# Two transformer blocks on one core: the first layer's modulation made per tile of x

## What is computed

```python
def _layer(x, c, positions, norm_g, w_ada, b_ada, w_in, ...):
    mod = jax.nn.silu(c) @ w_ada + b_ada
    shift, scale, gate = jnp.split(mod, 3, axis=-1)
    h = _rmsnorm(x, norm_g) * (1.0 + scale[:, None, :]) + shift[:, None, :]
    proj = h @ w_in
    (rq, rk, rv, rg, xbc, dt_raw, z, fq, fk, fv, fg, f_raw) = jnp.split(proj, IN_OFFSETS, axis=-1)
    ...
```

## Time and profile before

| | us |
|---|---|
| median of 3 runs | 3177.47 (3176.85 to 3179.08) |
| the profiled execution | 3176.42 |
| its span in the trace | 3174.6 |
| PE busy | 3070.6 |

### The profile page before, as it was taken

How to read it: one execution, slowest core, us unless ns; L and a number is a source line. 1 busy time by engine, 2 the same in 40 slices (tenths; PEclk the granted TensorE clock), 3 DMA queues, 4 the chain that set the end, 5 groups by cost and what they waited for, 6 DMA issues and landing times. The chain is left out here.

```text
span 3174.6 us, 39298 instructions
## 1 busy us (share of the span) xinstructions
PE 3070.6 (97%) x15352; PEld 2478.9 (78%) x15352; DVE 1241.9 (39%) x1997; ACT 928.7 (29%) x1623; POOL 1391.7 (44%) x1074
## 2 busy tenths in 40 slices
PE   8999999989999999999999999999999999999998
PEld 5887777778777788887767888878888776788886
DVE  8466244746433222222375322332222237532233
ACT  4356442435453211103463211021110346421101
POOL 2443445524343545445341544454444434154542
PEclk8999999999999999999999999999999999999999
DMA  6222315213231222232110222222222221022222
GB/s 262 100 82 105 101 57 210 103 67 113 87 110 40 73 101 92 85 97 95 67 41 28 93 97 93 91 90 101 98 85 92 86 80 41 28 92 93 88 91 72
DMA packets 45861, 287.78 MB, mean 91 GB/s; under 512 B 5496, under 2 KB 6008, under 8 KB 18680
## 3 DMA queue, kind: packets, MB, share of 16 engines
q1 hardware_dynamic: 42480, 270.32, 24.2%
q10 hardware_dynamic: 3240, 15.53, 1.5%
HBM read 283.67 MB, written 2.16 MB: 90 GB/s over the span
## 5 line engine op out<-in xcount | busy, mean ns | idle before, releaser
L1926 POOL TENSOR_TENSOR w_parts<-w_raw,w_parts 128x512 fp32r<-128x512 f32 (+1 forms) x544 | 703.2, 1321 | 752.9 <-DVE w_parts L2061 702.4
L1986 PE MATMUL PS<-x_parts,w_parts 128*128 128x512 f32 x4224 | 961.1, 390 | 4.5 <-ACT x_parts L799 4.5
L1986 PEld LDWEIGHTS PS<-x_parts,w_parts 128*128 128x128 f32 x4224 | 793.4, 188 | 173.7 <-issue 5.3
L139 POOL TENSOR_TENSOR w_parts<-w_raw,w_parts 128x512 fp32r<-128x512 f32 x380 | 532.6, 1432 | 820.4 <-ACT w_parts L128 790.6
L369 PE MATMUL PS<-x_parts,w_parts 128*128 128x512 f32 x2784 | 698.6, 397 | 14.8 <-POOL w_parts L139 13.7
L369 PEld LDWEIGHTS PS<-x_parts,w_parts 128*128 128x128 f32 x2784 | 521.2, 189 | 135.5 <-POOL w_parts L139 17.8
L2027 PE MATMUL PS<-hidden_parts,w_parts 128*128 128x512 f32 x2112 | 482.9, 390 | 0.0
L2027 PEld LDWEIGHTS PS<-hidden_parts,w_parts 128*128 128x128 f32 x2112 | 396.2, 188 | 83.8 <-issue 1.9
L2068 DVE TENSOR_TENSOR ffn_buffers<-PS,ffn_buffers 128x512 f32<-128x512 f32 x88 | 60.9, 692 | 732.1 <-PE PS L1986 708.9
L128 ACT CAST w_parts<-w_raw 128x2048 fp32r<-128x2048 f32 (+1 forms) x92 | 172.1, 1870 | 140.6 <-PE PS L369 52.3
L2061 DVE CAST w_parts<-w_raw 128x2048 fp32r<-128x2048 f32 (+1 forms) x144 | 156.9, 1089 | 113.4 <-PE PS L2027 113.4
(11 more groups left out here) (396 smaller groups left out, 3116.2 us busy)
## 6 DMA issues: line engine op xcount, KB each, us to landing
w_raw<-in_w_gu SPq DMA_DIRECT2D x88, 1024.0 KB, 4.7
w_raw<-in_w_in SPq DMA_DIRECT2D x70, 1024.0 KB, 4.8
w_raw<-in_w_d SPq DMA_DIRECT2D x64, 704.0 KB, 4.0
w_raw<-in_w_out SPq DMA_DIRECT2D x24, 1024.0 KB, 4.8
m_all<-in_w_next SPq DMA_DIRECT2D x14, 1024.0 KB, 8.2
m_all<-in_w_gate SPq DMA_DIRECT2D x8, 1024.0 KB, 4.8
ssd_buffers<-decay_rows ACTq DMA_DIRECT2D x16, 512.0 KB, 3.9
m_all<-in_w_next ACTq DMA_DIRECT2D x2, 1024.0 KB, 14.1
```

The source lines that it names most:

```text
L139: last = pool.tensor_tensor(parts[:, self.slot(u), 1, at:to], raw[:, self.slot(u), at:to], parts[:, self.slot(u), 0, at:to].bitcast(F32), ...
L1926: last = pool.tensor_tensor(WP[:, b, 1, at:to], RAW[:, b, at:to], WP[:, b, 0, at:to].bitcast(F32), ALU.subtract)
L1986: return pe.matmul(PS[:, 2 * b + g, :], WP[:, slot(b), w, c:c + P], XS[:, x, k, :], start=start, stop=stop)
```

## The change

Only the start of layer 0 changes; layer 1 goes on using `Modulated` and `begin`.

- The host lays the first-half weights of `w_ada` in layer 0 out anew: unit k now holds the shift and the scale of tile k of x. Units 0 to 2 (`TURNED` = 3) are stored the other way round for PE.
- Units 0 to 2 become products on PE (`product`): 16 matmuls of one column each per unit, with `c` as a column. Product 0 stands between the sums and `spread_inverse`, product 1 ahead of the first matmuls of jobs 0 and 1, product 2 ahead of those of the second tile.
- Units 3 to 7 stay dot products on DVE, now each ahead of its own tile, inside the loop over tiles.
- `begin_apart` begins four jobs on the arriving tiles: jobs 0 and 1 on tile n, jobs 2 and 3 on tile n - 3.
- The loads are ordered anew: x in two halves on both queues, c as a column and as a row, units 0 and 1 of `w_in` at once. The second `keep_busy` group and the two matmuls of `spread_inverse` go. The sines are made after the last tile.

```diff
-                self.spread_inverse(pe, 2)
-                keep_busy(pe, 2, 4)
+
+            def spread_inverse(self, pe):
+                pe.wait_ge(self.moved, 1)
+                for c in range(NT):
+                    last = pe.matmul(PS[:, RSTD, c * P:(c + 1) * P], stats[:, 8 + c:9 + c].broadcast_to([P, P]),
+                                     ident, start=True, stop=True)
+                last.then_inc(self.spread, 1)
...
+            def product(self, n):
+                def run(pe):
+                    pe.wait_ge(self.loaded[n], 16)
+                    if n == 0:
+                        pe.wait_ge(self.column_ready, 1)
+                    if n >= 2:
+                        pe.wait_ge(self.columns, 2 * (n - 1))
+                    for h in range(2):
+                        for k in range(KD):
+                            at = k * 2 * P + h * P
+                            last = pe.matmul(PS[:, self.bank(n), h:h + 1], self.ring[:, n, at:at + P],
+                                             self.c_column[:, k:k + 1], start=(k == 0), stop=(k == KD - 1))
+                    last.then_inc(self.products, 1)
+                return run
+
+            def vector(self, dve):
+                n = self.norm
+                dve.wait_ge(n.spread, 2)
+                for k in range(KD + 1):
+                    if k < KD:
+                        if k < TURNED:
+                            dve.wait_ge(self.products, k + 1)
+                            shift, scale = (PS[:, self.bank(k), h:h + 1] for h in range(2))
+                        else:
...
+                            dot_rows(dve, self.ring[:, k % 4, :], self.B.scratch, self.B.c_row,
+                                     raw_mod[:, 2 * k:2 * k + 2], self.used, 2 * m)
+                            dve.wait_ge(self.used, 2 * m + 2)
...
+                        dve.tensor_tensor(msb[:, k:k + 1], shift, p1("b_ada")[:, k:k + 1],
+                                          ALU.add).then_inc(self.columns, 1)
+                        dve.scalar_tensor_tensor(amul[:, k:k + 1], scale, msb[:, 8 + k:9 + k],
+                                                 p1("norm_g")[:, k:k + 1], ALU.add, ALU.mult).then_inc(self.columns, 1)
...
+                        dve.scalar_tensor_tensor(self.tile(k), X[:, k, :], amul[:, k:k + 1], PS[:, RSTD, :],
+                                                 ALU.mult, ALU.mult).then_inc(n.scaled, 1)
...
-                proj.begin(pe, (0, 1), before)
-                for j in range(2, nj):
+                if l:
+                    proj.begin(pe, (0, 1), before)
+                else:
+                    proj.begin_apart(pe, (((0, 1), 0), ((2, 3), 3)), before,
+                                     {n: before.product(n + 1) for n in range(TURNED - 1)})
+                for j in range(2 if l else 4, nj):
...
             def _(pe):
                 pe.wait_ge(s_in, 32)
                 norm.sums(pe, B.squares)
+                first.product(0)(pe)
+                norm.spread_inverse(pe)
...
+                act.dma_start(first.c_column, dr["c_column"]).then_inc(s_cc, 16)
                 act.dma_start(posi, dr["pos"]).then_inc(s_in, 16)
...
+                act.dma_start(x_all[:, half:2 * half], dr["x"][:, half:2 * half]).then_inc(s_x, 16)
+                act.dma_start(par[:, 0:P1N], of_layer("par1", 0)).then_inc(first.parameters, 16)
+                for u in range(2):
+                    act.dma_start(first.ring[:, u, :], ada_rows(0, u)).then_inc(first.loaded[u], 16)
+                act.dma_start(B.c_row, dr["c_row"]).then_inc(first.row_loaded, 16)
+                act.dma_start(first.ring[:, 2, :], ada_rows(0, 2)).then_inc(first.loaded[2], 16)
```

More of the change, by code:

```diff
@@ L316, in run_half, with begin_apart @@
                 last.then_inc(self.projected, 1)
+            def begin_apart(self, pe, groups, x, between):
+                for n in range(KD + 1 + max(lag for _, lag in groups)):
+                    if n in between:
+                        between[n](pe)
+                    for jobs, lag in groups:
+                        i = n - lag
+                        if 0 <= i < KD:
+                            pe.wait_ge(x.high, i + 1)
+                            for j in jobs:
+                                u, kind, c, m, ncols, kt = self.jobs[j]
+                                if i == 0:
+                                    pe.wait_ge(self.stream.low, u + 1)
+                                for a in range(2):
+                                    w = WP[:, self.stream.slot(u), a, 0:kt * ncols].rearrange("p (k n) -> p k n", k=kt)
+                                    pe.matmul(PS[0:m, self.bank(j), :], w[:, i, c:c + m], XS[:, 0, i, :],
+                                              start=(i == 0 and a == 0), stop=False)
+                        if 1 <= i <= KD:
+                            pe.wait_ge(x.low, i)
+                            for j in jobs:
+                                u, kind, c, m, ncols, kt = self.jobs[j]
+                                w = WP[:, self.stream.slot(u), 0, 0:kt * ncols].rearrange("p (k n) -> p k n", k=kt)
+                                last = pe.matmul(PS[0:m, self.bank(j), :], w[:, i - 1, c:c + m], XS[:, 1, i - 1, :],
+                                                 start=False, stop=(i == KD))
+                                if i == KD:
+                                    last.then_inc(self.projected, 1)
             def begin(self, pe, jobs, x, order=range(KD)):
@@ L2780, in mix_tokens, with setup @@
             return output
[L2783 to L2789, removed]
+        def setup(block, norm, B, first):
+            stream = first.stream
+            s_in, s_x = (sem(x) for x in ("constants_loaded", "x_loaded"))
+            s_cc = sem("c_column_loaded")
+            s_vc = sem("setup_vector_step")
@@ L2807, in _ @@
-                stream.send(sp, RAW, SLOTS)
-                sp.wait_ge(s_c1, 16)
+                    if u - 4 < TURNED:
+                        sp.wait_ge(first.products, u - 3)
+                    else:
+                        sp.wait_ge(first.used, 2 * (u - 3 - TURNED))
+                    sp.dma_start(first.ring[:, u % 4, :], ada_rows(0, u)).then_inc(first.loaded[u % 4], 16)
+                sp.dma_start(spec[:, 0:C1N], dr["c1"]).then_inc(first.constants, 16)
+                sp.wait_ge(first.constants, 16)
```

108 lines of the change are left out of this document (66 added, 42 removed).

## The result

| | before | changed |
|---|---|---|
| median of the runs, us | 3178.22 (3176.85 to 3179.08) | 3201.28 (3199.67 to 3204.27) |
| the profiled execution | 3176.42 | 3199.67 |
| its span | 3174.6 | 3197.9 |

The changed kernel is slower: the ratio is 1.0074, with a 95% interval of 1.0062 to 1.0087. The forecast was 3204, its range 3193 to 3212.

A forecast was written before the change was run, and what follows sets the result against it. PE, busy 97% of the span, was taken as the bound, so only the start mattered. Job 4 25.0 us later plus 2.0 of lost clock made 27.0; on 3176.4 plus 1.05 to the median, 3204 us, range 3193 to 3212.

The forecast's parts named there:

- The sum: Total predicted delay: job 4 starting 25.0 us later plus 2.0 us of lost clock, 27.0 us.
- Sums, products, spread at half clock: PE before tile 2: sums 11.57 us, each product 6.9 at 1.2 GHz, spread 2.08; tile 2 scaled at 52.2.
- The first landing: Constants and positions landing at the start, letting PE and DVE begin: 7.0 us, between 5.5 and 8.4.
- the squares: Eight squares of x at the start, 4.25 us, done by about 14.5 and hidden by PE's matmuls on constants.
- The tiles: Five tiles with two dots each on DVE, 4.5 us per tile, 22.5 in all, DVE the bound at full clock.
- rival B: Clock stays at 1.2 GHz through the tiles, so PE with 12 matmuls per tile is the bound: 3210 us; 15%.
- From the first evacuation to job 4: Chain of evacuation, rounding and POOL's low part kept whole at 12.8 us, plus 0.4 waiting for unit 2.
- PE's idle time: PE idle 8.7 us ahead of job 4, then at half clock, costing 2.0 us more (between 0 and 2.5).
- some 2 us either way: Bound given for where later gaps find the clock; not a term added to the total.
- Rival A: Clock stays at 2.4 GHz through sums and products, 3.8 us a product, 15.2 us less: 3189 us; 10%.
- Rival C: Cheap one-column matmuls at a pitch of 0.03 us make the change gain 2.4 us: 3175 us; 3%.
- D: Stages after job 4 give the delay back, whole: 3178 us; 3%.

## Why the prediction was right

The mechanism and the sign held, and the size to within 3 us. Part of that closeness is luck. The sum was 27.0 us, and the profiled executions are 23.3 apart: 2.4 us of the difference lie before job 4, where errors both ways partly cancel; 0.3 the other way are the clock behind it; 2.3 came back in later stages and 0.7 were lost behind the output, and the sum had no row for either. By its own steps:

- **Sums, products, spread at half clock.** Predicted 6.9 us a product, measured 6.97, 6.83 and 6.82; the three stand apart, as said, and the clock fell at 19 to 20. The sums were over-sized: 10.05 instead of 11.57. They had 2.4 GHz for some 4 us before it fell, where the sums before had under 3. The first landing was under-sized, 7.8 instead of 7.0, since the estimate looked at bytes and not at the small load ahead. x was down at 12.8 and not at about 10, so the squares ran from 12.88 to 17.13 instead of ending by 14.5; that cost nothing, as the sums (from 15.35) ran beside them without a gap. Tile 2 was scaled at 50.40 instead of 52.2.
- **The tiles.** 4.18 us instead of 4.5, five times: 1.6 us. The two dots took the 2.5 us that were priced. For the other four instructions I had added gaps; in the trace the next one starts about 0.08 us before the one ahead has ended. PE held 1.00, so rival B fell. The last tile was scaled at 71.32 instead of 74.7.
- **From the first evacuation to job 4.** 14.1 us instead of 13.2: the wait for unit 2 was 0.96 instead of 0.4, and POOL's low part of unit 2 with the release took 7.6 instead of 7.2. Job 4 at 89.5 instead of 91.9.
- **PE's idle time.** 9.4 us instead of 8.7; it cost 2.3 us of clock instead of 2.0.
- **Behind job 4.** The sum had let all 27 us through; 24.9 arrived there and 2.3 were given back: the two later half-clock stretches that were not met gave 1.6 and 1.4 us, and 0.7 of it was lost again elsewhere. That is the one term without a row in the sum, and it was named only as "some 2 us either way".

Rival A fell twice: the clock was at 0.50, and where wide matmuls held it, the products did run at 0.118 us an instruction. By the rule that the Trainium skill gives in TensorE: Matmul & The Clock Gate, section "HAM oscillation — how this bites in real kernels", idle gaps lose the clock; the idle stretch ahead of job 4 agrees (0.57 at 84 to 85 us), the sums and products, lost without a gap, are not covered by it. Rival C fell with the products at 6.9. D came true for a tenth of its size. The early begin of jobs 2 and 3, priced at nothing, was worth nothing (89.58 against 89.49).

## What to carry to other kernels

Ask of an early start what the next thing in line waits for: here four jobs began early and the fifth waited for the same chain, so that only the chain's first link, the last tile, set the time. Price a matrix-vector product on PE by its instructions and at the clock that it will have: here, with nothing wide among them, all but the first 4 us ran at the half-clock pitch. When a load is moved back in a queue, look at what the engine that waits for it has queued behind that wait. And when a chain on POOL is brought forward, look at what DVE does at that time: its instructions took 1.6 us instead of 0.7 beside it.

## What was not expected of the hardware

- Back-to-back one-column float32 matmuls let the granted clock fall from 1.00 to 0.50 with PE never idle. With a 512-column matmul after every four of them it held at 1.00 for 72 us; after every eight it fell as with none.
- A float32 matmul of 512 columns costs 0.80 us at 2.4 GHz (two instructions), nearly twice the 0.43 us that I had counted for it.
- A 4 KB load of 128 rows of 32 bytes, first in its queue, put off the landing behind it by 2.8 us (7.77 against 4.99); behind large loads it took 13.3 us itself.
- Among the tiles, 4.18 us apart, the clock stayed at 1.00 with four begun jobs. In the one profile with two it fell twice, to 0.50 at 60 to 63 us and again at 74 to 76.
- Beside POOL's subtractions a 128x512 instruction on DVE took 1.63 us instead of 0.69, and in two executions a single one took 12.88 us.
- At the start the profile's clock column can mislead: it shows 1.00 from 8 to 12 us in the changed kernel, ahead of the first change that it records, while the weight loads of the constants come 0.85 us apart (9.66, 10.51, 11.37) and later, in the same loop, 0.43 us apart (13.64, 14.06, 14.49).
